# RWKV chunk inverse: each doubling level carries A X and its transpose, in one group of products

## The reference, cut to what matters

```python
def step(state, inp):
    rt, lwt, kt, vt, at, bt = inp
    sa = jnp.einsum('bhvk,bhk->bhv', state, at)
    state = (state * jnp.exp(lwt)[:, :, None, :] + sa[..., None] * bt[:, :, None, :]
             + vt[..., None] * kt[:, :, None, :])
    return state, jnp.einsum('bhvk,bhk->bhv', state, rt)
```

## Time and profile before

| what | us |
|---|---|
| median of 3 runs | 2707.01 (2706.76 to 2708.63) |
| the profiled execution | 2708.32 |
| its span in the trace | 2706.6 |
| PE busy | 2557.6 |
| DVE busy | 1124.8 |
| ACT busy | 817.4 |

### The profile page before, as it was taken

The page is one execution under the profiler, slowest core; times in us unless marked ns, Lnnn a source line. Parts: engine busy times, 40 slices in busy tenths (PEclk is TensorE's granted clock), DMA queues, the critical chain, the costliest instruction groups (busy, mean ns, idle before and its releaser), DMA issues.

```text
span 2706.6 us, 40099 instructions
## 1 busy us (share of the span) xinstructions
PE 2557.6 (94%) x15677; PEld 1717.8 (63%) x15677; DVE 1124.8 (42%) x1631; ACT 817.4 (30%) x1010; POOL 105.6 (4%) x136
## 2 busy tenths in 40 slices
PE   7999999999999999999999999799899988899896
PEld 5888888877777777777788887343333333333342
DVE  5333334344556665566444222333323322333334
ACT  5433344433434444344222222112111111112112
POOL 0000000000000000000000000000000000000000
PEclk9999999999999999999999999799999999999998
DMA  5333333333222222223744533999999999999995
GB/s 167 98 104 108 108 104 98 98 97 91 70 77 70 81 81 79 69 78 86 231 143 139 177 109 117 395 420 422 421 421 422 421 421 422 422 422 421 422 421 229
DMA packets 312381, 594.38 MB, mean 220 GB/s; under 512 B 17098, under 2 KB 238918, under 8 KB 260550
## 3 DMA queue, kind: packets, MB, share of 16 engines
q1 hardware_dynamic: 303372, 559.71, 56.4%
q0 software_dynamic: 8912, 33.22, 3.1%
HBM read 578.02 MB, written 24.64 MB: 223 GB/s over the span
## 4 chain that ended last, share of the span: by engine, by line
PE 78%; DMA 15%; DVE 3%; issue 1%; ACT 1%; SPq 0%; DVEq 0%; ACTq 0%
PE in_z L160 36%; DMA ex_w_up<-in_expert_w_up_dram 15%; PE bank L2370 11%; PE bank L2397 4%; PE bank L2357 1%; PE mg_z_rw L151 1%; PE mg_z_rw L152 1%; PE mg_z_rw L150 1%; PE in_z L151 1%; PE in_z L152 1%; PE in_z L150 1%; PE rw_b L1299 1%; PE rw_b L1290 1%; PE bank L2358 1%; DVE in_lo L192 1%
## 5 line engine op out<-in xcount | busy, mean ns | idle before, releaser
L160 PE MATMUL in_z<-xn_hi,in_lo 128*128 128x512 f32 x1440 | 582.9, 405 | 0.0
L160 PE MATMUL in_z<-xn_hi,in_hi 128*128 128x512 f32 x1440 | 568.8, 395 | 5.3 <-DVE in_lo L192 3.8
L160 PE MATMUL in_z<-xn_lo,in_hi 128*128 128x512 f32 x1440 | 564.0, 392 | 0.0
L2370 PE MATMUL bank<-ex_w_gate,ex_xt_sb 128*64 128x512 f32 x768 | 360.3, 618 | 51.8 <-DMA ex_w_up<-in_expert_w_up_dram 51.7
L192 DVE TENSOR_TENSOR in_lo<-in_raw,in_hi 128x2048 fp32r<-128x2048 f32 x122 | 281.6, 2308 | 272.1 <-ACT in_hi L187 155.8
L2372 PE MATMUL bank<-ex_w_up,ex_xt_sb 128*64 128x512 f32 x768 | 361.1, 620 | 0.0
L160 PEld LDWEIGHTS in_z<-xn_hi,in_hi 128*128 128x128 f32 x1440 | 271.2, 188 | 66.3 <-issue 8.6
L160 PEld LDWEIGHTS in_z<-xn_hi,in_lo 128*128 128x128 f32 x1440 | 270.7, 188 | 60.1 <-issue 3.4
L160 PEld LDWEIGHTS in_z<-xn_lo,in_hi 128*128 128x128 f32 x1440 | 270.7, 188 | 58.7 <-issue 1.9
L2370 PEld LDWEIGHTS bank<-ex_w_gate,ex_xt_sb 128*64 128x64 f32 x768 | 105.1, 142 | 275.6 <-issue 275.5
L2397 PE MATMUL bank<-ex_w_down,const 128*64 128x512 f32 x512 | 229.3, 601 | 2.6 <-issue 0.9
(11 more groups left out here) (501 smaller groups left out, 3455.5 us busy)
## 6 DMA issues: line engine op xcount, KB each, us to landing
ex_w_down<-in_expert_w_down_dram SPq DMA_DIRECT2D x128, 1024.0 KB, 20.7
ex_w_gate<-in_expert_w_gate_dram SPq DMA_DIRECT2D x96, 1024.0 KB, 21.7
ex_w_up<-in_expert_w_up_dram SPq DMA_DIRECT2D x96, 1024.0 KB, 24.9
in_raw<-in_w_in_dram SPq DMA_DIRECT2D x91, 1024.0 KB, 5.7
in_raw<-in_w_out_dram SPq DMA_DIRECT2D x32, 512.0 KB, 4.7
ex_w_gate0b<-in_expert_w_gate_dram SPq DMA_DIRECT2D x16, 1024.0 KB
ex_w_up0b<-in_expert_w_up_dram SPq DMA_DIRECT2D x16, 1024.0 KB
rt_then_ex_w<-in_expert_w_gate_dram SPq DMA_DIRECT2D x16, 1024.0 KB
```

The source lines that it names most:

```text
L160: return pe.matmul(out, w[:, k, :], x[:, k, :], start=(n == 0), stop=(n == PASSES * KT - 1), skip_group_check=True)
L2370: pe.matmul(gate_up[low, :], x_t[:, k, halves[u]], w_gate[n][u][:, j, :], start=start, stop=stop, skip_group_check=True)
```

## The change

Each level now works on A X and its transpose, instead of on X. Before the levels, 16 products form A X and 16 more its transpose (the operands exchanged). In each level DVE masks A X and adds the identity (`step`, two instructions in place of one mask); ACT copies the transpose to `ax_t`; then one group of 16 products gives the next A X, and a second group, right behind it, the next transpose. The last level has only the first group. At the end DVE forms X as I + A X in one instruction. The four transposes and the masked product of each level go. The operands alternate between the array's row halves and column halves from level to level (`here`, `there`). `step` shares memory with `kbd`. Between the levels' groups stand now (7, 7, 13, 7, 7) dense passes, 41 in all, where there were nine times 6, 54 in all. No other line of the order changes.

```diff
     DECAY = float(np.exp(-0.5))
-    DVE_STEPS = 26
+    DVE_STEPS = 31
     ACT_STEPS = 3
...
         QUADS = N_CHUNKS // 2
-        (kb_r, kb), (kbd_r, kbd) = (mem.shared((f"rw_{n}_r", [P, 2, T], F32R), ("rw_" + n, [P, QUADS, 4, RW_CHUNK], F32))
-                                    for n in ("kb", "kbd"))
+        kb_r, kb = mem.shared(("rw_kb_r", [P, 2, T], F32R), ("rw_kb", [P, QUADS, 4, RW_CHUNK], F32))
+        kbd_r, kbd, step = mem.shared(("rw_kbd_r", [P, 2, T], F32R), ("rw_kbd", [P, QUADS, 4, RW_CHUNK], F32),
+                                      ("rw_step", [P, 2, 2, QUADS, RW_CHUNK], F32))
         ar = mem.sb("rw_ar", [P, N_CHUNKS, 2, RW_CHUNK])
...
         x_mat = mem.sb("rw_x_mat", [P, QUADS, 2, RW_CHUNK])
-        x_tr = mem.sb("rw_x_tr", [P, QUADS, P])
+        ax_t = mem.sb("rw_ax_t", [P, 2, QUADS, RW_CHUNK])
         state = tm[:].rearrange("p i q t -> p (i q) t")
...
             "tok_done", "tok_by_act", "tok_by_dve", "mats_done", "mats_ready")
-        xm_ready, xtr_done, x_ready, t_done, t_ready, xmul_done = sems.sem(
-            "xm_ready", "xtr_done", "x_ready", "t_done", "t_ready", "xmul_done")
+        xm_ready, ax_done, ax_t_done, ax_t_ready, step_ready = sems.sem(
+            "xm_ready", "ax_done", "ax_t_done", "ax_t_ready", "step_ready")
+        AX = len(LEVELS) + 1
         tail_done, tail_by_act, tail_by_dve, s_done, s_ready = sems.sem(
...
                 for lv in range(len(LEVELS)):
-                    act.wait_ge(xtr_done, 5 * p + lv + 1)
-                    act.activation(x_tr[:], twin[0][:, 0, :].rearrange("p (q s) -> p q s", s=P), ACT.Copy).then_inc(x_ready, 1)
+                    act.wait_ge(ax_t_done, len(LEVELS) * p + lv + 1)
+                    act.activation(ax_t[:], head_major(twin[2]), ACT.Copy).then_inc(ax_t_ready, 1)
                     if lv == 0 and not last:
...
                 for lv in range(len(LEVELS)):
-                    dve.wait_ge(t_done, 5 * p + lv + 1)
-                    tt(tm[:], head_major(twin[1]), pairs_of(steps[lv]), ALU.mult).then_inc(t_ready, 1)
-                    dve.wait_ge(xmul_done, 5 * p + lv + 1)
-                    tt(x_mat[:], x_mat[:], head_major(twin[2]).rearrange("p h q t -> p q h t"), ALU.add).then_inc(xm_ready, 1)
+                    dve.wait_ge(ax_done, AX * p + lv + 1)
+                    order.done(tt(step[:, lv % 2], head_major(twin[1]), pairs_of(steps[lv]), ALU.mult))
+                    order.wait()
+                    every = step[:, lv % 2].rearrange("p a q t -> p (a q) t")
+                    tt(every, every, eight(ident64, RW_CHUNK), ALU.add).then_inc(step_ready, 1)
                     if lv == (0 if last else 1):
...
                         tt(bonus_parts[1], bonus[:], bonus_parts[0].bitcast(F32), ALU.subtract).then_inc(sum_lo, 1)
+                dve.wait_ge(ax_done, AX * p + AX)
+                tt(x_mat[:], head_major(twin[1]).rearrange("p h q t -> p q h t"),
+                   ident64.rearrange("p (a b t) -> p a b t", a=1, b=1).to_broadcast([P, QUADS, 2, RW_CHUNK]), ALU.add
+                   ).then_inc(xm_ready, 1)
                 dve.wait_ge(tail_done, PE_TAIL * p + AKV)
...
                 dense(19)
-                at_level = (6,) * len(LEVELS)
+                wait_apart(pe, keep["pe_waits"], xm_ready, 2 * p + 1)
+                wait_apart(pe, keep["pe_waits"], mats_ready, 2 * p + 2)
+                units = [(c, c // 2, 1 - c % 2, h) for c in range(N_CHUNKS) for h in range(2)]
+                for c, q4, m, h in units:
+                    mm = pe.matmul(twin[1][halves[h], m, quad(c)], gs[halves[m], h, c, FOR_A, :], x_mat[halves[m], q4, h, :],
+                                   start=True, stop=True, skip_group_check=True)
+                mm.then_inc(ax_done, 1)
+                for c, q4, m, h in units:
+                    mm = pe.matmul(twin[2][halves[h], m, quad(c)], x_mat[halves[m], q4, h, :], gs[halves[m], h, c, FOR_A, :],
+                                   start=True, stop=True, skip_group_check=True)
+                mm.then_inc(ax_t_done, 1)
+                at_level = (7, 7, 13, 7, 7)
                 for lv in range(len(LEVELS)):
-                    pe.wait_ge(xm_ready, 6 * p + lv + 1)
-                    for q4 in range(QUADS):
-                        mm = pe.transpose(twin[0][:, 0, P * q4:P * q4 + P], x_mat[:, q4, :, :], ident)
-                    mm.then_inc(xtr_done, 1)
-                    wait_apart(pe, keep["pe_waits"], mats_ready, 2 * p + 2)
-                    for c in range(N_CHUNKS):
-                        q4, m = c // 2, 1 - c % 2
-                        for h, rows in enumerate(halves):
-                            mm = pe.matmul(twin[1][rows, m, quad(c)], gs[halves[m], h, c, FOR_A, :], x_mat[halves[m], q4, h, :],
+                    dense(at_level[lv])
+                    wait_apart(pe, keep["pe_waits"], ax_t_ready, len(LEVELS) * p + lv + 1)
+                    wait_apart(pe, keep["pe_waits"], step_ready, len(LEVELS) * p + lv + 1)
+                    here, there = ((lambda m, h: h), (lambda m, h: m))[::1 - 2 * (lv % 2)]
+                    for c, q4, m, h in units:
+                        rows, k = halves[here(m, h)], there(m, h)
+                        mm = pe.matmul(twin[1][halves[k], here(m, h), quad(c)], ax_t[rows, k, q4, :], step[rows, lv % 2, k, q4, :],
+                                       start=True, stop=True, skip_group_check=True)
+                    mm.then_inc(ax_done, 1)
+                    if lv < len(LEVELS) - 1:
+                        for c, q4, m, h in units:
+                            rows, k = halves[here(m, h)], there(m, h)
+                            mm = pe.matmul(twin[2][halves[k], here(m, h), quad(c)], step[rows, lv % 2, k, q4, :], ax_t[rows, k, q4, :],
                                            start=True, stop=True, skip_group_check=True)
-                    mm.then_inc(t_done, 1)
-                    dense(at_level[lv])
-                    wait_apart(pe, keep["pe_waits"], t_ready, 5 * p + lv + 1)
-                    wait_apart(pe, keep["pe_waits"], x_ready, 5 * p + lv + 1)
-                    for c in range(N_CHUNKS):
-                        q4, m = c // 2, 1 - c % 2
-                        for h, rows in enumerate(halves):
-                            mm = pe.matmul(twin[2][halves[m], h, quad(c)], x_tr[rows, q4, RW_CHUNK * m:RW_CHUNK * m + RW_CHUNK],
-                                           tm[rows, m, q4, :], start=True, stop=True, skip_group_check=True)
-                    mm.then_inc(xmul_done, 1)
-                    dense(at_level[lv] if lv < len(LEVELS) - 1 else 0)
+                        mm.then_inc(ax_t_done, 1)
 
...
                 dense(4)
-                wait_apart(pe, keep["pe_waits"], xm_ready, 6 * p + 6)
+                wait_apart(pe, keep["pe_waits"], xm_ready, 2 * p + 2)
                 for h in range(2):
...
```

## The result

The changed kernel takes 2737.8 us (median of 4 runs, 2736.4 to 2738.5) against 2707.7 of the kernel before on the same chip: ratio 1.0108, 95% interval 1.0096 to 1.012. It is 30 us slower, where +24 was forecast; the range of 2716 to 2742 holds it. The profiled execution took 2737.95, its span is 2736.3.

A forecast was written before the change was run, and what follows sets the result against it. PE was taken to bound the RWKV stage, at full clock without gaps. Regular pairs: -3.07 + 0.2 + 4.3 + 1.7 = +3.1 us, seven +22; last pair +2; in all +24, 2731 us, range 2716 to 2742.

The forecast's parts named there:

- PE's own work in the levels: First A X group to AKV: 16.72 us with lead-in passes against 22.74 before, gain 3.07 us a pair.
- ACT and DVE in the levels: Seven passes cover both engines; PE waits 0.2 us in level 2, about 1.5 in the last pair.
- The mean's wait: Behind the levels, PE's mean waits 4.3 us for ACT's copies in each of seven regular pairs.
- The clock: Behind each new wait PE's clock falls to half for 3.4 us, costing 1.7 us a time.
- the wait is deeper: Rival: clock stays low twice as long in most pairs, up to 7 x 1.7 us more, 2743; chance 0.04.
- The last pair: Merge load lands later, first merge pass 6.3 us late against 2.7 before; with the other terms +2 us.
- The stages behind: Stages behind the RWKV stage start that much earlier or later, one for one.

The follow-up runs named there:

- e3: Changed kernel with the 13 dense passes put back in the levels, ahead of the last level's group, (7, 7, 13, 7, 20); 2687.4 us, ratio 0.9917.
- e4: Kernel before, old levels kept but with 13 dense passes fewer in them, which come at the pair's end; 2762.6 us, ratio 1.0205.
- e5: Changed kernel with 18 surplus PE products ahead of the mean's wait in the seven regular pairs, result unread; 2721.0 us.
- e6: Changed kernel with 54 passes in the levels, (7, 7, 13, 7, 20) in regular pairs, (7, 13, 7, 7, 20) in the last; 2687.5 us, ratio 0.9928.
- e8: Changed kernel with seven of the thirteen passes back in the levels, (7, 7, 13, 7, 14); 2711.9 us, ratio 1.0012.

## Why the prediction was right, point by point

- **PE's own work in the levels.** Forecast 16.62 us from the first A X group to AKV and 0.2 of wait in it, measured 16.66 with 0.18. Gain forecast at 3.07 - 0.2 = 2.9 a pair; e3, where it stands alone, shows 3.0. The floor of about 25 ns from matmul to matmul in the Trainium skill ("TensorE: Matmul & The Clock Gate", section "Back-to-back issue gap") would have made a group 0.8 us; L1306 to L1312 is 0.51 us for 32 records. The row decided rightly.
- **ACT and DVE in the levels.** Seven passes cover both. The last pair's wait was forecast at 1.5 and is 1.54 in e3's trace and in the changed kernel's.
- **The mean's wait.** Forecast 4.3 us in seven pairs, measured 4.26. The 192nd pass is the eighth of the twelve, ACT's chain is 4.92 us long as before (4.93), and e3 and e4 show that the shift of the borders makes it.
- **The clock.** The mechanism was right and its size was not. I took 1.7 us a time, half of the 3.4 us in the earlier trace rows, and gave as the reason that both rows were of shorter idle times; that reason speaks for a longer fall, not for the same. In the changed kernel the clock was low for 6.8 us in six of the seven pairs, as the stretch from 808.70 on shows:

```profile
806.00:808.60 2.60, 0.00 (x0) 0.00 (x0) 1.76 (x1) 2.57 (x3) 0.00 (x0) 1.00 0.00 0
808.70:815.50 6.80, 5.63 (x11) 3.84 (x12) 1.73 (x3) 3.00 (x5) 0.55 (x1) 0.51 0.68 195
```

It fell some 3 us into the idle time, while PE still waited, and 5.6 us of work fell under it: 2.7 us by PE's timeline, 2.6 by e5. The rival "the wait is deeper" had the duration (twice as long in most pairs) but priced it at 3.4, as if all the low time were work. In pair 0 the clock was low for 3.4 us, and there the price was the forecast's: 88.2 us less e3's 82.3 and the wait of 4.26 leaves 1.7. So this term is mis-sized by 0.9 us in six pairs, 5 us. The levels and the wait, each a little cheaper than forecast, give back 1, and the regular pairs hold 4 of the 6 us that the forecast was short.
- **The last pair.** Forecast +2.0, measured +2.3, which is near in part by luck. The load was sized too late: the first merge pass was to be 6.3 us late, and ran at 1346.93, after 4.92 us of idle PE and 5.1 us behind its due time, since the load took 12.7 us where I had 14.0. Two terms that I didn't have make up for it: the stop of 0.5 us in a group of the levels (see e6), and some 0.5 us of clock, which was low for 6.8 us there against 3.4 before. The waits view names DVE's low split as the releaser of the merge pass. That split is the next unit's (split(5)), for which this pass doesn't wait; in the kernel before it ran only at 1319.14, behind the first merge pass at 1317.39. The second half of the merge load ends closer to the pass: it was issued at 1334.14 and took 12.7 us, as this line of the DMA issues (KB of one, us to landing) of the stretch has it, so it landed at 1346.84, 0.09 us ahead of the pass. So PE waits for the load, as forecast, going by the code and the times; no run took the load away.

```profile
y_lo<-scratch_y_split SPq DMA_DIRECT2D x1, 2048.0 KB, 12.7
```

- **The stages behind.** Forecast to shift one for one. They did but for 1.4 us (1.7 in the expert stage, -0.2 in the routing), which the runs do not explain.

The sum of the parts agrees with the whole: -3.0 (e3) + 4.3 + 2.6 (e5) = +3.9 a pair, and the pairs are 88.9 against 85.0.

## What to carry to other kernels

Where work is interleaved by hand, moving filler from one place to another moves every border of the filler against the chain. So follow each thing that waits for a border (here a ring slot's release on ACT, and on DVE behind it) and list what stands behind it in that engine's order, before asking whether the new place has enough cover. A change that shortens one section of a chain should keep the borders where they were until its gain is measured alone: here the shorter levels are worth 22 us, and thirteen passes of 0.23 us in another place cost 50.

When a wait of PE is priced, add the work that runs at the low clock behind it.

## What the runs showed of the hardware that was not expected

- The same idle time may or may not lower TensorE's clock. In e8 PE waits 2.5 to 2.6 us in each pair, and the granted clock falls in pairs 0, 1, 3 and 5 and stays up in 2, 4 and 6; the difference is 1.5 us of time. With 4.1 us of idle time it fell in all seven pairs of the changed kernel and of e4, but not for as long: 3.4 us in one pair and 6.8 in six, and in e4 3.4 in four and 6.8 in three.
- A table load on ACT cost what its record says. The Trainium skill, "ScalarE: Activation LUTs", section "What ACT_TABLE_LOAD costs", gives about 1.28 us for the load and 1.38 more for a drain at every switch. In ACT's timeline of pair 1 above the load starts 0.02 us behind the hi split's end, lasts 1.28, and the next activation starts 0.01 behind it: no drain shows. By the page's figure, an estimate, the chain would be 1.4 us longer with one.
